# Two orders of the SBUF buffers in a two-block transformer forward pass

## The reference

```python
def first_block(h, ...):                   # two layers
    h = h + hybrid_attention_mixer(rms_norm(h, ...), ...)     # dilated and differential heads
    h = h + conv_ffn(rms_norm(h, ...), ...)                   # width 3072, gated, conv of 3
    h = h + recurrent_mixer(rms_norm(h, ...), ...)            # conv of 4, gates, linear scan
    h = h + conv_ffn(rms_norm(h, ...), ...)
def hybrid_layer(x, ...):                  # second_block: two of these, then a norm
    x = x + jnp.sum(gates * proj, axis=2) @ w_o               # three attentions and a conv of 31
    x = x + jnp.square(jax.nn.relu(hf @ w_up)) @ w_down       # width 4096
```

## Time and profile before

| what | value |
|---|---|
| median of three runs | 2974.97 us |
| the profiled execution's own time | 2973.88 us |
| its span, first to last instruction | 2972.1 us |
| mean granted TensorE clock | 0.979 |
| TensorE matmul busy | 2832.8 us, 95% |
| VectorE busy | 1388.6 us, 47% |
| ScalarE busy | 1231.8 us, 41% |
| GpSimd busy | 1231.3 us, 41% |

### The profile page before, as it was taken

How to read it: one execution, slowest core, us unless ns; L and a number is a source line. 1 busy time by engine, 2 the same in 40 slices (tenths; PEclk the granted TensorE clock), 3 DMA queues, 4 the chain that set the end, 5 groups by cost and what they waited for, 6 DMA issues and landing times.

```text
span 2972.1 us, 31436 instructions
## 1 busy us (share of the span) xinstructions
PE 2832.8 (95%) x12424; PEld 2250.3 (76%) x12424; DVE 1388.6 (47%) x2084; ACT 1231.8 (41%) x1797; POOL 1231.3 (41%) x550
## 2 busy tenths in 40 slices
PE   8897999999879999999899999999998999999998
PEld 6554788888667888877577888888875778888886
DVE  3896651444876515434955353012329553431113
ACT  3574442343644424433474344233235743342331
POOL 4221344444453444443454444444433544444442
PEclk9998999999989999999899999999998999999999
DMA  4211222222222322222112222232221123222222
GB/s 150 78 58 42 76 95 100 92 100 99 71 71 85 100 99 93 99 92 92 37 66 84 97 95 98 94 99 100 97 87 44 65 71 100 99 93 99 99 93 77
DMA packets 73922, 259.15 MB, mean 87 GB/s; under 512 B 9184, under 2 KB 9184, under 8 KB 73776
## 3 DMA queue, kind: packets, MB, share of 16 engines
q1 hardware_dynamic: 71680, 251.79, 25.3%
q10 hardware_dynamic: 2096, 5.36, 0.5%
HBM read 254.95 MB, written 2.13 MB: 86 GB/s over the span
## 4 chain that ended last, share of the span: by engine, by line
PE 81%; DVE 12%; issue 3%; ACT 3%; POOL 1%; DMA 0%; DVEq 0%; ACTq 0%; POOLq 0%
PE ps L376 25%; PE ps L378 25%; PE ps L377 25%; DVE pbuf L1272 1%; PE ps L440 1%; DVE pbuf L1250 1%; PE ps L470 1%; DVE tmp L1316 1%; PE ps L422 1%; PE ps L385 1%; PE ps L424 1%; PE ps L423 1%; POOL w_lo L1726 1%; PE ps L453 1%; DVE att L1641 1%
## 5 line engine op out<-in xcount | busy, mean ns | idle before, releaser
L1726 POOL TENSOR_TENSOR w_lo<-raw,w_hi 128x1024 fp32r<-128x1024 f32 x470 | 1135.2, 2418 | 1575.3 <-ACT w_hi L791 1575.0
L376 PE MATMUL ps<-xs,w_hi 128*128 128x512 f32 x2304 | 912.5, 396 | 16.5 <-POOL w_lo L1726 9.5
L378 PE MATMUL ps<-xs,w_lo 128*128 128x512 f32 x2304 | 899.2, 390 | 0.0
L377 PE MATMUL ps<-xs,w_hi 128*128 128x512 f32 x2304 | 899.1, 390 | 0.0
L791 ACT ACTIVATE w_hi<-raw 128x1024 fp32r<-128x1024 f32 x470 | 494.0, 1053 | 688.2 <-PE ps L378 644.3
L376 PE MATMUL ps<-hid,w_hi 128*128 128x512 f32 x1320 | 524.9, 398 | 33.8 <-DVE hid L1177 11.4
L376 PEld LDWEIGHTS ps<-xs,w_hi 128*128 128x128 f32 x2304 | 434.2, 188 | 116.0 <-POOL w_lo L1726 12.2
L377 PE MATMUL ps<-hid,w_hi 128*128 128x512 f32 x1320 | 520.5, 394 | 0.0
L378 PE MATMUL ps<-hid,w_lo 128*128 128x512 f32 x1320 | 520.1, 394 | 0.0
L377 PEld LDWEIGHTS ps<-xs,w_hi 128*128 128x128 f32 x2304 | 434.2, 188 | 92.6 <-issue 4.3
L378 PEld LDWEIGHTS ps<-xs,w_lo 128*128 128x128 f32 x2304 | 433.9, 188 | 91.7
(11 more groups left out here) (193 smaller groups left out, 2306.7 us busy)
## 6 DMA issues: line engine op xcount, KB each, us to landing
raw<-in_weights SPq DMA_DIRECT2D x470, 512.0 KB, 3.4
hT<-in_x ACTq DMA_DIRECT2D x4, 512.0 KB, 9.7
btab<-in_rel SPq DMA_DIRECT2D x8, 256.0 KB, 3.7
out<-tmp ACTq DMA_DIRECT2D x8, 256.0 KB, 2.0
btab<-in_heads SPq DMA_DIRECT2D x6, 256.0 KB, 3.9
tmp<-in_heads SPq DMA_DIRECT2D x6, 256.0 KB, 3.8
common<-in_fixed ACTq DMA_DIRECT2D x1, 642.0 KB, 14.0
small<-in_small ACTq DMA_DIRECT2D x1, 368.5 KB, 5.0
```

Of the source, the lines that this page charges most:

```text
L376: pe.matmul(banks[bank][:], wh, rh, start=(k == 0), stop=False)
L377: pe.matmul(banks[bank][:], wh, rl, start=False, stop=False)
L378: last = pe.matmul(banks[bank][:], wl, rh, start=False, stop=(k == len(specs) - 1))
L1726: gp.tensor_tensor(w_lo[:, n % NPAIR, :], raw[:, n % NRAW, :], w_hi[:, n % NPAIR, :].bitcast(F32), ALU.subtract).then_inc(*w_low.tick(n))
```

## The change

The order of the `sb(...)` calls is another one. No size, type, instruction, operand slice, wait or semaphore is touched: in the two built programs each engine has the same instructions in the same order, and they differ in the start addresses of the SBUF buffers alone.

```diff
--- before.py
+++ after.py
@@ -133,29 +133,28 @@
 
         w_in = nc.dram_tensor("in_weights", [NSLAB, P, SLAB], F32, kind="ExternalInput").ap()
         scratch = nc.dram_tensor("forget", [4, S], F32).ap()
-
-        fgt = sb("fgt", [P, 6, 16])
-        tiny = sb("tiny", [P, 256])
         hT = sb("hT", [P, 8, S])
         xs = sb("xs", [P, 16, S], F32R)
+        raw = sb("raw", [P, NRAW, SLAB])
+        w_hi = sb("w_hi", [P, NPAIR, SLAB], F32R)
+        w_lo = sb("w_lo", [P, NPAIR, SLAB], F32R)
+        small = sb("small", [P, nsmall])
+        common = sb("common", [P, 1284])
+        ones = sb("ones", [P, 4, P])
+        aug = sb("aug", [P, 2, S])
+        btab = sb("btab", [P, 2, S])
+        pt = sb("pt", [P, 2, 4, S])
+        pbuf = sb("pbuf", [P, 6, S])
+        tmp = sb("tmp", [P, 10, S])
+        tiny = sb("tiny", [P, 256])
+        fgt = sb("fgt", [P, 6, 16])
+        rp = sb("rp", [P, S])
+        rt = sb("rt", [P, S])
+        spb = sb("spb", [P, 5, 8])
+        hb = sb("hb", [P, 16])
         with nc.sbuf_tensor("att", [P, 32, S], F32) as att:
             pass
         hid = sb("hid", [P, 32, S], F32R)
-        pt = sb("pt", [P, 2, 4, S])
-        raw = sb("raw", [P, NRAW, SLAB])
-        w_hi = sb("w_hi", [P, NPAIR, SLAB], F32R)
-        w_lo = sb("w_lo", [P, NPAIR, SLAB], F32R)
-        pbuf = sb("pbuf", [P, 6, S])
-        aug = sb("aug", [P, 2, S])
-        btab = sb("btab", [P, 2, S])
-        tmp = sb("tmp", [P, 10, S])
-        rp = sb("rp", [P, S])
-        rt = sb("rt", [P, S])
-        ones = sb("ones", [P, 4, P])
-        common = sb("common", [P, 1284])
-        small = sb("small", [P, nsmall])
-        spb = sb("spb", [P, 5, 8])
-        hb = sb("hb", [P, 16])
         banks = [ctx.enter_context(nc.psum_tensor(f"ps{i}", [P, S], F32)) for i in range(8)]
 
         ident = common[:, 0:128]
```

## The result

The changed order takes 3000.15 us, the median of four runs (2999.54 to 3001.33), against 2975.43 us for the order before, the median of four runs too (the three known before and one more). The ratio is 1.0084, with a 95% interval of 1.0066 to 1.0101. So it is 24.7 us slower. The prediction was 2975 us, with a range up to 2989. The profiled execution took 2999.06 us, with a span of 2997.3 us, 25.2 us over that of before.

A forecast was written before the change was run, and what follows sets the result against it. The prediction took the pace of TensorE's matmuls, plus its waits for the vector engines, as the bound. It added zero for matmuls, other engines and loads to 2973.88 us, set 2975 for the median, range 2969 to 2989.

The forecast's parts named there:

- the matmul term: TensorE's matmuls on `hid`, 3960 of them: bounded between 13.6 us slower and 55 us faster, taken as zero.
- TensorE reads `hid` more slowly: Matmuls on `hid` from first output projection to last stage get slower; 13.6 us, so 2989; chance 0.12.
- The sign that the prediction named for it: Mean of matmul line L376 on `hid` above 398 ns while on `xs` it stays at 396.
- VectorE's shifted taps: Nearest rows with a shift: 4 to 120 bytes cost a few ns at most, used for taking zero on TensorE.
- The upper bound: Matmuls on `hid`: 32 bytes off cost eight more columns, 3.4 ns each, 13.6 us over 3960.
- The rival of the 14 ns: Matmuls on `hid` lose the 14 ns over their columns' time; 55 us faster, 2920 in full; chance 0.04.
- Zero for the other engines, the loads and the clock: VectorE, ScalarE, GpSimd and weight loads add zero; the clock counts 3 us either way.
- an estimate of 0.1 us more for a load: Weight loads land in 3.5 us instead of 3.4; 47 us if one behind the other, nothing under the cover.

The follow-up runs named there:

- e2: Order before with `att` and `hid` 32 bytes further, all other buffers at their remainders to 512; 3000.90 us, ratio 1.0084.
- e3: Order before with `w_hi` and `w_lo` 32 bytes further, all other buffers at their remainders; 3035.75 us, ratio 1.0201.
- e7: Order before with `xs` alone 32 bytes further, all other buffers at their remainders; 3017.73 us, ratio 1.0137.
- e5: Order before with `xs` and all buffers behind it, including `hid` and the weights, 32 bytes further; 2976.91 us, ratio 1.0004.
- e1: Changed order with 32 unused bytes ahead of `att` and `hid`, so `hid` starts at a multiple of 64; 2986.32 us, ratio 1.0035.
- e11: Order before with `att` and `hid` 28 bytes further; 2984.00 us, ratio 1.0031.
- e9: Matmuls alone, without the model: operand pairs at starts 0 and 32, fixed and in turn, and other widths; matching pairs in turn took 560 periods.
- e13: Matmuls alone, without the model: narrower stationary operands, alternating operands, the kernel's sequence; 544, 554, 544, 560 periods for 32, 64, 96, 128 columns at distance 32.

## Why the prediction was wrong

The step that failed is the matmul term, "I take zero". It measured 6.5 ns by 3960 matmuls, 25.7 us, and made the result; e2, in which only `hid` moves, by the same 32 bytes, repeats it. What stands in place of the zero is a dependence of the fp32r matmul's pace on how the starts of its two operands lie to each other. The rival "TensorE reads `hid` more slowly" was the right place, the right count and the right sign. Its chance was 0.12, and its price of 13.6 us was about half of what came. The sign that the prediction named for it is what the page of after shows: L375 on `hid` at 403 ns, on `xs` at 396.

- *The evidence was taken from the wrong engine.* I let VectorE's shifted taps speak for TensorE. They spoke truly for VectorE: after the change its times stand. They say nothing of an engine whose pace hangs on two operands. Before, all of TensorE's fp32r operands lay at a distance of 0, so no row could price another distance. With no row, the chance should have been spread wider.
- *The upper bound was mis-sized.* Eight columns, 3.4 ns, was a picture of one stream that reads a little more. The measured excess is 6.5 ns at 32 bytes and 10 to 12 at 4 bytes. A bound from a picture is not a bound from rows, and the high end of the range, 2989, rested on it.
- *The rival of the 14 ns had the right pair and the wrong sign.* I named weights and activations that "start at the same place within 512 bytes" as the possible cause of the 14 ns over the columns' time. Starts that agree are the good case. I also argued that an excess paid once a matmul doesn't look like two streams in each other's way. The 16 periods at 512 columns do come from the relation of two operands, and at 256 columns the same 32 bytes save 8 periods, so neither a fixed cost nor one per column describes it.
- *Zero for the other engines, the loads and the clock was right.* Busy times agree within 2.5 us, landings at 3.4 us, the clock at 0.93 in attention. From the Trainium skill's rule on descriptors that don't start at a multiple of 256 bytes ("DMA: Bandwidth & Descriptors", how a descriptor splits into AXI transactions) the prediction had an estimate of 0.1 us more for a load; the median landing, 3.4 us in both, doesn't show it.
- *The sum for whole buffers runs high where attention is touched.* e3 moved 10872 + 384 spacings by about 6.4 ns, 72 us, and cost 59; e7 moved 6912 + 384 by 6.3 ns, 46 us, and cost 42. In e3 the share of TensorE in the chain that ended last rose from 81 to 83% and VectorE's fell from 12 to 10%. That fits matmuls that got longer inside stretches which VectorE bounded before, but no run tested it. The mean granted clock, 0.980 in e3 against 0.979, could give back 3 us at most.

The Trainium skill, in "SBUF — State Buffer", section "Who interferes with whom", gives TensorE two read ports, one for the streamed operand and one for the weights, and calls them independent. That is hard to square with the fp32r matmuls here: e2, e3 and e5 differ only in where the two operands lie, and run at 560, 560 and 544 periods.

What stays open is the mechanism below the distance: why the curve has its shape over 256 bytes, why crossed pairs in turn take 568, why a scan backwards gives other values at 108, 188 and 236 bytes, why the three passes differ in e1 and e11, and why `hid` at 28 and at 4 bytes is 5 and 3 periods worse in the kernel than in the measurement alone.

## What to carry to other kernels

When fp32r matmuls of 512 columns run back to back, with 128 stationary columns, place all weights and activations so that their starts have the same remainder to 256 bytes; here it was worth 0.84% for one activation buffer (`hid`) and 2.0% for both. All of them must agree with each other: in e9 pairs that match each for itself, at 0 and at 32, took 560 periods in turn. For narrower matmuls measure first, since e9 and e13 have other distances as the best ones. Look for it in the count of matmuls in a stretch that is 100% busy, since busy share and waits don't show it. Where a change moves addresses and the trace has only one arrangement of them, keep a wide range, and don't let one engine's indifference vouch for another's. Don't rely on a single measured value of the curve either: 28 bytes were free alone and cost 8 us in the kernel.

## What the runs showed of the hardware

- The spacing of fp32r matmuls of 512 columns with 128 stationary columns depends on the distance of the two operands' starts: 544 periods of 2.4 GHz at 0 and at 256, 560 at 32, up to 576 (at 120 among others), and under 544 at no distance. The forward scan repeats after 256 bytes.
- At a distance of 0 the absolute start doesn't matter to within 2 periods: 544 at 0 on 0, 544 to 546 at 32 on 32 and at 128 on 128, and 2976.91 us for a kernel with all three buffers off 64 bytes.
- The distance isn't all: at 108 bytes a forward scan had 544 periods and a backward one 560, and the stationary operand at 4 and 16 bytes took 558 and 560 where the scan has 545 and 544.
- It is not an alignment rule: 64 and 128 bytes of distance cost 5 and 16 periods, 28 and 60 bytes none in the measurement alone.
- bf16 (518 periods) and plain fp32 (1030) are the same at every distance tried (0, 4, 32, 64 and 128).
- In all eleven layouts the other engines kept their times: the fastest of VectorE's L1192 took 736 to 741 ns, the median tap 738 to 741, ScalarE's pass over a slab 1052 to 1055 and GpSimd's 2412 to 2422 in the mean, and the median weight load landed in 3.4 to 3.5 us.
